# Retention heads: the norm's sums by one product with ones, root and reciprocal per token on all partitions, and a second load of the sample tokens' keys and values

## The reference, cut to what matters

```
def retention_chunkwise(q, k, v, s0, chunk):       # prompt: chunks of 128, samples: chunks of 8
    ...
        att = jnp.einsum('bihd,bjhd->bhij', qc, kc) * dmat[None]
        o = jnp.einsum('bhij,bjhe->bihe', att, vc) + jnp.einsum('bihd,bhde->bihe', qc, s) * q_decay
        s = s * chunk_decay + jnp.einsum('bjhd,bjhe->bhde', kc * k_decay, vc)
def retention_out(o, gate):
    y = o * lax.rsqrt(jnp.mean(o * o, axis=-1, keepdims=True) + EPS)
    return y.reshape(B, L, H * dv) * jax.nn.silu(gate.astype(F32))
```

## Time and profile before

| | |
|---|---|
| median of 3 executions | 3076.86 us (3075.38 to 3077.79) |
| the profiled execution | 3080.52 us, of which the span is 3077.9 us |
| PE busy | 98% of the span |
| DVE, ACT, POOL busy | 41%, 25%, 5% |
| mean granted clock of PE | 0.990 of full speed |
| DMA | mean 116 GB/s |

### The profile page before, as it was taken

One profiled execution on the slowest core, in us unless ns is written; L12 is line 12 of the kernel. 1 busy time (PEld: TensorE's weight loads), 2 busy tenths in 40 slices (PEclk: granted clock), 3 DMA queues, 4 the chain that ended last, 5 costly groups with the idle time before them and its releaser, 6 DMA issues.

```text
span 3077.9 us, 48517 instructions
## 1 busy us (share of the span) xinstructions
PE 3017.6 (98%) x20106; PEld 2754.6 (89%) x20106; DVE 1272.6 (41%) x1895; ACT 779.1 (25%) x946; POOL 149.6 (5%) x254
## 2 busy tenths in 40 slices
PE   7999999999999999998999999999999999999998
PEld 7899999999899998777989889899898898998977
DVE  5544245455554445557333333333333233233235
ACT  6311123322322233434212112112121121121222
POOL 0000012312211000000000000000000000000000
PEclk9999999999999999999999999999999999999999
DMA  5433535545656453423222222222222222222232
GB/s 184 158 105 109 149 119 162 165 141 167 212 160 232 146 194 102 138 69 117 87 82 77 92 73 82 92 73 93 82 77 86 77 86 82 81 82 82 82 144 89
DMA packets 366168, 356.21 MB, mean 116 GB/s; under 512 B 9446, under 2 KB 296412, under 8 KB 363900
## 3 DMA queue, kind: packets, MB, share of 16 engines
q1 hardware_dynamic: 344696, 269.18, 28.6%
q0 software_dynamic: 21152, 85.70, 8.2%
q10 hardware_dynamic: 228, 0.06, 0.0%
HBM read 306.67 MB, written 48.23 MB: 115 GB/s over the span
## 4 chain that ended last, share of the span: by engine, by line
PE 91%; issue 3%; DVE 2%; DMA 2%; ACT 1%; POOL 1%; DVEq 0%; POOLq 0%; ACTq 0%
PE gemm L2006 56%; PE aux L2613 7%; PE aux L2614 7%; PE aux L2615 7%; PE gemm L2618 2%; PE gemm L2617 2%; PE aux L2115 1%; PE gemm L2092 1%; PE aux L2006 1%; PE aux L2155 1%; PE aux L2171 1%; DMA g_row<-in_norm_mlp_post 1%; PE gemm L2035 0%; DVE y_tok L1947 0%; POOL d_kp L714 0%
## 5 line engine op out<-in xcount | busy, mean ns | idle before, releaser
L2006 PE MATMUL gemm<-act_hi,w_hi 128*128 128x288 f32 x4512 | 988.5, 301 | 7.3 <-DVE yT L1662 3.6
L2006 PE MATMUL gemm<-act_hi,w_lo 128*128 128x288 f32 x4512 | 968.1, 296 | 0.0
L2006 PE MATMUL gemm<-act_lo,w_hi 128*128 128x288 f32 x4512 | 967.2, 296 | 0.0
L2006 PEld LDWEIGHTS gemm<-act_hi,w_hi 128*128 128x128 f32 x4512 | 726.7, 189 | 39.1 <-issue 23.5
L2006 PEld LDWEIGHTS gemm<-act_lo,w_hi 128*128 128x128 f32 x4512 | 728.8, 189 | 0.0
L2006 PEld LDWEIGHTS gemm<-act_hi,w_lo 128*128 128x128 f32 x4512 | 728.7, 189 | 0.0
L1246 DVE TENSOR_TENSOR w_lo<-w_raw,w_hi 128x2048 fp32r<-128x2048 f32 x214 | 490.0, 2290 | 467.1 <-ACT w_hi L1191 325.9
L2613 PE MATMUL aux<-w_hi,u_hi 128*128 128x512 f32 x1024 | 399.8, 390 | 6.3 <-DVE w_lo L1246 6.3
L2614 PE MATMUL aux<-w_hi,u_lo 128*128 128x512 f32 x1024 | 399.0, 390 | 0.0
L2615 PE MATMUL aux<-w_lo,u_hi 128*128 128x512 f32 x1024 | 398.9, 390 | 0.0
L1191 ACT ACTIVATE w_hi<-w_raw 128x2048 fp32r<-128x2048 f32 x63 | 120.6, 1914 | 539.5 <-PE aux L2615 539.5
(11 more groups left out here) (343 smaller groups left out, 2010.5 us busy)
## 6 DMA issues: line engine op xcount, KB each, us to landing
w_raw<-in_w_mlp_up SPq DMA_DIRECT2D x64, 1024.0 KB, 6.4
w_raw<-in_w_mlp_down SPq DMA_DIRECT2D x64, 1024.0 KB, 5.0
w_raw<-in_w_in SPq DMA_DIRECT2D x56, 1024.0 KB, 5.7
w_raw<-in_w_out SPq DMA_DIRECT2D x16, 1024.0 KB, 5.8
z_scratch<-z_out SPq DMA_DIRECT2D x56, 288.0 KB, 2.1
r_zin<-z_scratch POOLq DMA_DIRECT2D x8, 1152.0 KB, 6.8
d_z<-z_scratch POOLq DMA_DIRECT2D x12, 576.0 KB, 7.1
xin<-in_x_prompt POOLq DMA_DIRECT2D x6, 1024.0 KB, 7.7
```

What stands on the lines that cost most here:

```text
L2006: ins = M(out[half][:, 0:TH], w[b][:, cols], x[:, k, half * TH:(half + 1) * TH], start=first and n == 0, stop=last and n == 2)
```

## The change

The squares are summed by one product with a 128x128 matrix of ones, so the sum of each token stands on every partition. ACT's root and DVE's reciprocal then run over 128x576 values, and `r_diag` and the product `bc` go. `y1` and `y1s` stand ahead of the reciprocal; one `y2` over all 576 tokens follows it directly, ahead of the copy of the finished tile (`z_ret` in head 3, `part_take(4k+1)` in heads 4 to 7) and of `lo`. The next head's PE work waits for `y1s` and `rts` in place of `y2s`. For the samples, POOL loads the 64 key and value columns twice side by side into `r_two` by two more DMAs per head (64 KB each, in pieces of 256 bytes), so that `st` is two full transposes.

```
-        r_rms = sb("r_rms", [P, NT], F32, st)
-        r_diag = sb("r_diag", [P, T], F32, st)
+        r_rms = sb("r_rms", [P, T], F32, st)
...
                 pool.dma_start(r_zin[h % 2][:], zr[h]).then_inc(r_zin_full[h % 2], 16)
+                for i in range(2):
+                    pool.dma_start(r_two[h % 2][:, :, i, :], zr[h][:, 1:3, TP:T]).then_inc(r_zin_full[h % 2], 16)
...
-                R_ACT.did(nc.scalar.activation(r_rms[:, 0:PC], A[0][:, TS:TS + PC], ACT.Sqrt, bias=eps[:], scale=1.0 / P), "rt")
+                R_ACT.did(nc.scalar.activation(r_rms[:, 0:TP], A[1][:], ACT.Sqrt, bias=eps[:], scale=1.0 / P), "rt")
...
-                R_ACT.did(nc.scalar.activation(r_rms[0:TS, PC:NT], A[0][0:TS, TS + PC:TS + NT], ACT.Sqrt,
-                                               bias=eps[0:TS, :], scale=1.0 / P), "rts")
+                R_ACT.did(nc.scalar.activation(r_rms[:, TP:T], A[2][:, 0:TS], ACT.Sqrt, bias=eps[:], scale=1.0 / P), "rts")
...
-                dve.wait_ge(r_zin_full[h % 2], 16 * (h // 2 + 1))
+                dve.wait_ge(r_zin_full[h % 2], 48 * (h // 2 + 1))
...
-                after(R_ACT, "rts", h)
-                ready("rcp")
-                own("rcp", V.reciprocal(r_rms[:, 0:PC], r_rms[:, 0:PC]))
-                ready("rcps")
-                own("rcps", V.reciprocal(r_rms[0:TS, PC:NT], r_rms[0:TS, PC:NT]))
-                ready("diag")
-                own("diag", V.tensor_tensor(r_diag[:, 0:TP].rearrange("p (c t) -> p c t", c=PC), ident.unsqueeze(1).to_broadcast([P, PC, P]),
-                                            r_rms[:, 0:PC].unsqueeze(2).to_broadcast([P, PC, P]), ALU.mult))
-                ready("diags")
-                own("diags", V.tensor_scalar(r_diag[0:TS, TP:T], ident[0:TS, 0:TS], r_rms[0:TS, PC:NT], None, ALU.mult))
+                after(R_ACT, "sqs", h)
                 ready("y1")
                 own("y1", V.tensor_tensor(r_y[:, 0:TP], A[3][:], r_gate[:, 0:TP], ALU.mult))
                 ready("y1s")
                 own("y1s", V.tensor_tensor(r_y[:, TP:T], A[0][:, 0:TS], r_gate[:, TP:T], ALU.mult))
+                after(R_ACT, "rts", h)
+                ready("rcp")
+                own("rcp", V.reciprocal(r_rms[:], r_rms[:]))
+                after(R_DVE, "rcp", h)
+                own("y2", V.tensor_tensor(r_y[:], r_y[:], r_rms[:], ALU.mult))
                 if h == RF - 1:
                     z_ret(first, 0, 16 * (first // 2), first % 4, (first - ZD) // 4 * 2 + first % 4)
                 if h < RF:
...
                 else:
                     part_take(4 * (h - RF) + 1)
                     lo(S_OUT + 2 * (h - RF) + 2, 0)
-                after(R_PE, "bc", h)
-                ready("y2")
-                own("y2", V.tensor_tensor(r_y[:, 0:TP], r_y[:, 0:TP], A[1][:], ALU.mult))
-                ready("y2s")
-                own("y2s", V.tensor_tensor(r_y[:, TP:T], r_y[:, TP:T], A[2][:, 0:TS], ALU.mult))
...
-                    after(R_DVE, "y2s", h - 1)
-                pe.wait_ge(r_zin_full[h % 2], 16 * (h // 2 + 1))
+                    after(R_DVE, "y1s", h - 1)
+                    after(R_ACT, "rts", h - 1)
+                pe.wait_ge(r_zin_full[h % 2], 48 * (h // 2 + 1))
...
-                turn(A[2][0:TS, 0:P], r_k[:, TP:T])
-                turn(A[2][0:TS, P:2 * P], r_w[:, TP:T])
-                M(A[2][TS:P, 0:P], r_k[:, TP:T], ident, start=True, stop=True, tile_position=(0, TS))
-                R_PA.did(M(A[2][TS:P, P:2 * P], r_w[:, TP:T], ident, start=True, stop=True, tile_position=(0, TS)), "st")
+                for i in range(2):
+                    ins = turn(A[2][:, i * P:(i + 1) * P], r_two[h % 2][:, i, :, :].rearrange("p a t -> p (a t)"))
+                R_PA.did(ins, "st")
...
-                for c in range(NT):
-                    c0, rows = tok(c)
-                    ins = M(A[0][0:rows, TS + c:TS + c + 1], r_sq[:, c0:c0 + rows], ones[:, 0:1], start=True, stop=True)
-                R_PE.did(ins, "cs")
-                fill(5)
-                after(R_DVE, "diags", h)
-                M(A[1][:], ones[:], r_diag[:, 0:TP], start=True, stop=True)
-                R_PE.did(M(A[2][:, 0:TS], ones[0:TS, :], r_diag[0:TS, TP:T], start=True, stop=True), "bc")
-                fill(6, 7)
+                M(A[1][:], ones[:], r_sq[:, 0:TP], start=True, stop=True)
+                R_PE.did(M(A[2][:, 0:TS], ones[:], r_sq[:, TP:T], start=True, stop=True), "cs")
+                fill(5, 6, 7)
```

More of the change, by code:

```diff
@@ L285, in program @@
         r_v = sb("r_v", [P, NT, P], F32, st)
+        r_two = [sb(f"r_two{b}", [P, 2, 2, TS], F32, st) for b in range(2)]
         r_tab = [r_tab0, sb("r_tab1", [P, R_W], F32, st)]
@@ L413, in program @@
         R_ROT = Steps(sem("r_rot"), "u")
-        R_DVE = Steps(sem("r_dve"), "qd qp kd kds vs att atts vbd s0 s1 s2 s3 sn0 sn1 ot rcp rcps diag diags y1 y1s y2 y2s lo")
+        R_DVE = Steps(sem("r_dve"), "qd qp kd kds vs att atts vbd s0 s1 s2 s3 sn0 sn1 ot y1 y1s rcp y2 lo")
         R_ACT = Steps(sem("r_act"), "v gate sq sqs rt rts hi")
         R_PA = Steps(sem("r_pa"), "kt vt st att atts")
-        R_PE = Steps(sem("r_pe"), "m sn o ot os cs bc")
+        R_PE = Steps(sem("r_pe"), "m sn o ot os cs")
         r_zin_full = [sem(f"r_zin_full{b}") for b in range(2)]
@@ L1005, in r_head @@
                     split(S_OUT + 2 * (h - RF) + 2, G_OUT + 4 * (h - RF) + 2)
-                act.wait_ge(R_DVE.sem, R_DVE.of("y2s", h))
+                act.wait_ge(R_DVE.sem, R_DVE.of("y2", h))
                 if h < RF and h:
```

## The result

The changed kernel takes 3081.39 us against 3076.89 us before (medians of 22 runs each; ratio 1.0012, interval 1.0006 to 1.0017). That is 4.5 us more, 0.15%: within 0.2%, on the slow side. The forecast was 5.5 us more, 3082.4. The profiled execution has a span of 3079.7 us and a mean granted clock of 0.989.

A forecast was written before the change was run, and what follows sets the result against it. The prediction took PE, busy for 98% of the span, to bound the kernel. PE work -14.2, waits +13.4, clock +6.1 and loads +0.2 gave +5.5 us, so 3082.4 us, range 3075 to 3088.

The forecast's parts named there:

- PE loses work: Retention heads: dropped fp32 products, cheaper sums and one fewer interlude save 1.77 us per head, 14.2 us in all.
- a wait came up in heads 0 to 3: Sign against the prediction: heads 0 to 3 should last 35.0 us in place of 36.8, without a PE wait.
- DVE's chain: Norm in each head: roots of 0.69 and 0.31 us, reciprocal 3.74, `y2` 0.76; DVE gains about 2.3 us of work.
- The wait: Heads 4 to 7: `fill(6)` waits 3.25 us for the tile's copy, 3.35 with the first step, 13.4 us in all.
- no wait at all: Rival at `fill(6)`: no wait, needing a reciprocal under 0.6 us; all 14.2 us come off, 3062.7; chance 0.09.
- The clock: Heads 4 to 7: PE's clock falls behind each wait, commonly costing 1.5 us, 6.1 us in all, bounds 0 and 10.
- The long stretch: Behind a PE wait of 3.60 us the clock's low level held 6.8 us, priced at 2.5 us lost.
- The loads: Two more 64 KB DMAs per head on POOL's queue: at most head 0 is delayed, taken as 0.2 us.
- late bound: Head 0's new loads take 4.4 us, land at 806.5, wait 2.3 us; rival with clock 1.5: 3086, chance 0.05.
- read-modify-write below 512 bytes: The new loads' 256-byte pieces: by the skill page, head 0's landing nears the late bound, the sum 2 us higher.
- The sum: Whole kernel: -14.2 + 13.4 + 6.1 + 0.2 = +5.5 us, a median of 3082.4.

The follow-up runs named there:

- e1: Changed kernel with the finished tile's copy put back ahead of the wait for the root in heads 4 to 7: 3062.36 us; again on another occasion 3063.01.
- e3: Changed kernel without the second load, so only the new norm, with the old two transposes and two fp32 products for the samples: 3085.07 us.
- e2: Kernel before with only the second load of the samples' keys and values and the two full transposes: 3073.65 us.
- e6: e1 with the samples' sum of squares taken by a 64-row product over 64 of the 128 channels: 3065.8 us.
- e5: Kernel before with a reciprocal of an unread tile put ahead of the copy in heads 4 to 7, and one memset in head 2: 3093.09 us.
- e4: Changed kernel with the reciprocal of heads 4 to 7 over 288 of 576 columns: 3066.78 us.
- e7: Changed kernel with the reciprocal of heads 4 to 7 over 160 of 576 columns: 3064.87 us.
- e8: e1 with the samples' scores-times-values product on all 128 rows, the scores' lower half zero: 3060.83 us; 3059.7 on another chip.

## Why the prediction was right

**PE loses work: right, too small.** The forecast was 1.77 us per head; the clean head of e1 lasts 34.51 against 36.76, so 2.25, 18 us in all. The missing 0.48 can be split by e3 and e2. A clean head of e3 lasts 35.28 us, so the new norm saves 1.49 against a forecast of 1.19: 0.31 of that is the new `cs`, priced by `bc`'s 64-row product (shown by e6). The second load saves the other 0.76 against 0.58: 0.09 are the transposes (984.19 - 983.10 = 1.09 us in place of 1.18), and the scores behind them take 0.98 us in place of 1.09; why, no run shows. In heads 0 to 3 about 1.2 us went back: their lengths are 35.16, 34.76, 34.51 and 34.78. In head 0 PE waited 0.36 us for `r_kd`, which the shorter head start had run up to. The prediction said that it would be wrong if a wait came up in heads 0 to 3; this one did, and it is small. The other 0.8 us I haven't placed.

**DVE's chain: right.** Forecast 0.69, 0.31, 3.74 and 0.76 us; the rows give 0.69, 0.31, 3.75 and 0.76.
**The wait: right, its size to a few hundredths by luck.** Forecast 3.25 us at `fill(6)` of heads 4 to 7, released by the copy; measured 3.28, four times. e1 takes it away, e5 makes it without the change, e4 and e7 scale it. Two errors cancelled in its size. PE reached `fill(6)` 0.31 us sooner than forecast, since the new `cs` costs 1.00 us. From the start of the sums to the copy's end DVE and ACT took 974.98 - 967.41 = 7.57 us against a forecast of 7.89: the sums end 0.19 us sooner, and `y2` and the copy start with less than the gap that I allowed. (For no wait at all the reciprocal would have had to take under 0.5 us, 3.74 - 3.25, and not 0.6; nothing hangs on it.)

**The clock: right in kind and size.** It fell in each of the four heads of the profiled execution, three times for 3.4 us and once for 6.8; heads 4 to 6 last 4.8 to 5.0 us longer than 34.5, 3.4 of it the wait and the step behind it, 1.4 to 1.6 the clock. e4 against the changed kernel gives 1.9 per head, and four heads as profiled give 3 x 1.5 + 2.6 = 7.1 us, 1.8 per head, against the forecast's 6.1 in all. The long stretch doesn't go with the longer wait: behind the one at the end of the cross-attention, 3.60 us before and 3.62 in the changed kernel, the lower level lasted 6.8 us and 3.4.

**The loads: right.** No PE wait for them, e2 gains. The new loads landed 6.4 and 6.7 us after their issue and `r_zin` ahead of them 6.7 after its own. Of the read-modify-write below 512 bytes that the Trainium skill names ("DMA: Bandwidth & Descriptors", section "Specifications") no cost is seen in the time; no run has the same loads in longer pieces. (Twice 2.1 us are 4.2, and not the 4.4 of the late bound.)

**The sum.** -18.0 + 1.2 + 4 x 3.4 + 3 x 1.5 + 2.6 (the long stretch, priced as in the prediction) = +3.9 us in the profiled heads, against a measured +4.5. My -14.2 was 2.6 us too weak in net, the clock's 6.1 was 1.0 too small, and the 0.2 for the loads wasn't there. So the forecast of +5.5 lies within 1.0 us of the measurement partly because its errors point both ways. The 0.6 us between +3.9 and +4.5 are inside the spread of single runs (3073.4 to 3079.9 before). The two profiled executions differ by 1.8 us only: outside the retention heads and up to 3050 us the clock was at its lower level for 54.6 us in the one before and for 44.4 in the changed one.

## What to carry to other kernels

An engine at 40% can still be late once per stage: what counts is what stands behind a long instruction in its program, and how much slack its consumer had (here 0.8 us; counted from the sums' start, the copy ended 2.7 us later and PE came 1.4 us sooner). Put copies that free a busy engine's buffers ahead of anything that waits. A wait of 3.3 us on PE cost another 1.4 to 2.6 us through the clock here, and one of 1.5 us nothing, so shortening a wait can pay beyond its length.

## What was not expected of the hardware

A 64-row fp32 product of 64 columns between 128-row ones costs 0.36 us, a 128-row one 0.14 (e6), twice the work at less than half the price. The Trainium skill ("TensorE: Matmul & The Clock Gate", section "Step-by-step: what each phase is for") says that the row count doesn't matter for loading weights. In the load's own duration it hardly does here (0.184 us for 64 rows, 0.190 for 128); in when the load starts it does.

After a wait of 1.81 us the clock fell, after 2.86 us in three heads of four, after 3.28 in all four of the changed kernel but in three of e3; after 1.48 and 0.68 us it held in all eight heads of the profiled executions. Length alone doesn't decide it. One wait of the cross-attention is as long in the changed kernel as before; before, the clock fell behind it, and in the changed kernel it held. First the kernel before, then the changed one:

```profile
1294.42 2.67 PE L2492 MATMUL aux<-c_mkt,c_q 128*128 128x256 f32 x8 [2.26 <-ACT c_p L1128]
1295.00:1299.00 4.00, 4.00 (x15) 2.13 (x13) 3.26 (x10) 1.22 (x3) 0.00 (x0) 0.57 0.93 313
...
1298.27 1.99 PE L2478 MATMUL aux<-c_mkt,c_q 128*128 128x256 f32 x8 [2.25 <-ACT c_p L1129]
1298.00:1306.00 8.00, 6.96 (x44) 4.15 (x45) 4.45 (x13) 4.91 (x15) 0.00 (x0) 1.00 0.59 187
```

On `yT` it held after 1.77 us (e8) and 2.01 (e1, second time). Where the line lies these runs don't say.
